# Norm and first FFN tiles worked by halves of the tokens behind three output projections, and a reordered opening

## What is computed

```python
x = x + 0.5 * swiglu(rms_norm(x, ffn1_norm), ffn1_w_in, ffn1_w_out)
h = rms_norm(x, mix_norm); ...attention...
x = x + mix @ w_mix_out                                  # output projection 1
x = x + 0.5 * swiglu(rms_norm(x, ffn2_norm), ffn2_w_in, ffn2_w_out)
for l in range(2):
    sh1, sc1, g1, sh2, sc2, g2 = split(silu(c) @ mod_w[l] + mod_b[l], 6)
    h = h + g1 * attention(modulate(rms_norm_2(h, norm1_g[l]), sh1, sc1))  # output projections 2, 3
    h = h + g2 * conv_ffn(modulate(rms_norm_2(h, norm2_g[l]), sh2, sc2))
```

## Time and profile before

| | |
|---|---|
| median of 3 runs | 2302.79 us (2302.18 to 2304.47) |
| profiled execution, its own time | 2299.5 us |
| its span, first to last instruction | 2298.0 us |
| PE busy (matmuls) | 2223.4 us, 97% of the span |
| DVE busy | 1270.5 us, 55% |
| ACT busy | 950.2 us, 41% |
| mean granted TensorE clock | 0.986 |

### The profile page before, as it was taken

One profiled execution on the slowest core, in us unless ns is written; L12 is line 12 of the kernel. 1 busy time (PEld: TensorE's weight loads), 2 busy tenths in 40 slices (PEclk: granted clock), 3 DMA queues, 4 the chain that ended last, 5 costly groups with the idle time before them and its releaser, 6 DMA issues.

```text
span 2298.0 us, 31235 instructions
## 1 busy us (share of the span) xinstructions
PE 2223.4 (97%) x11568; PEld 1831.8 (80%) x11568; DVE 1270.5 (55%) x2069; ACT 950.2 (41%) x1460; POOL 268.2 (12%) x442
## 2 busy tenths in 40 slices
PE   7999999998999999999999999999989999999998
PEld 6788887977778888887878788888878887888886
DVE  5754764456743363355356656456466655654654
ACT  4222223347644323324246554254253645533542
POOL 2110220035400020010036000000000430000000
PEclk9999999998999999999999999999999999999999
DMA  7864983231033283273321233333212012323332
GB/s 245 275 210 122 317 289 96 92 103 38 11 117 102 87 281 108 79 256 118 96 76 59 73 91 96 106 84 89 86 63 82 30 38 74 91 92 100 91 96 87
DMA packets 258720, 266.92 MB, mean 116 GB/s; under 512 B 8854, under 2 KB 201917, under 8 KB 258637
## 3 DMA queue, kind: packets, MB, share of 16 engines
q1 hardware_dynamic: 236909, 187.20, 27.2%
q0 software_dynamic: 21728, 78.63, 9.9%
HBM read 263.62 MB, written 12.66 MB: 120 GB/s over the span
## 4 chain that ended last, share of the span: by engine, by line
PE 86%; DVE 6%; ACT 4%; DMA 1%; POOL 1%; issue 1%; DVEq 0%; SPq 0%; POOLq 0%; ACTq 0%
PE bank L340 15%; PE bank L341 15%; PE bank L342 15%; PE bank L346 11%; PE bank L348 11%; PE bank L347 11%; PE bank L1567 2%; PE bank L1518 2%; PE bank L1542 2%; DVE w_lo L323 1%; ACT probs L1603 1%; POOL probs L1725 1%; DMA mod_w_more<-in_mod_w_dram 1%; PE bank L667 1%; DVE xT_lo L642 1%
## 5 line engine op out<-in xcount | busy, mean ns | idle before, releaser
L323 DVE TENSOR_TENSOR w_lo<-raw,w_hi 128x2048 fp32r<-128x2048 f32 (+3 forms) x202 | 415.6, 2057 | 374.2 <-ACT w_hi L319 371.5
L340 PE MATMUL bank<-xT_hi,w_hi 128*128 128x512 f32 x1560 | 609.6, 391 | 6.1 <-DVE xT_lo L642 4.2
L342 PE MATMUL bank<-xT_hi,w_lo 128*128 128x512 f32 x1560 | 607.8, 390 | 0.0
L341 PE MATMUL bank<-xT_lo,w_hi 128*128 128x512 f32 x1560 | 607.8, 390 | 0.0
L319 ACT ACTIVATE w_hi<-raw 128x2048 fp32r<-128x2048 f32 (+3 forms) x202 | 348.4, 1725 | 484.0 <-PE bank L348 429.9
L340 PEld LDWEIGHTS bank<-xT_hi,w_hi 128*128 128x128 f32 x1560 | 292.5, 188 | 73.3 <-DVE xT_lo L642 8.8
L342 PEld LDWEIGHTS bank<-xT_hi,w_lo 128*128 128x128 f32 x1560 | 292.5, 188 | 62.3
L341 PEld LDWEIGHTS bank<-xT_lo,w_hi 128*128 128x128 f32 x1560 | 292.4, 187 | 60.0
L346 PE MATMUL bank<-w_hi,hid_hi 128*128 128x512 f32 x704 | 277.8, 395 | 0.0
L347 PE MATMUL bank<-w_lo,hid_hi 128*128 128x512 f32 x704 | 277.8, 395 | 0.0
L348 PE MATMUL bank<-w_hi,hid_lo 128*128 128x512 f32 x704 | 277.7, 395 | 0.0
(11 more groups left out here) (303 smaller groups left out, 2858.8 us busy)
## 6 DMA issues: line engine op xcount, KB each, us to landing
raw<-in_ffn_w_in_dram SPq DMA_DIRECT2D x40, 1024.0 KB, 6.1
raw<-in_f_win_dram SPq DMA_DIRECT2D x40, 1024.0 KB, 6.0
mod_w<-in_mod_w_dram POOLq DMA_DIRECT2D x48, 512.0 KB, 5.3
mod_w_more<-in_mod_w_dram POOLq DMA_DIRECT2D x48, 512.0 KB, 5.6
raw<-in_ffn_w_out_dram SPq DMA_DIRECT2D x24, 768.0 KB, 4.5
raw<-in_f_wout_dram SPq DMA_DIRECT2D x24, 768.0 KB, 4.4
raw<-in_a_wqkv_dram SPq DMA_DIRECT2D x12, 1024.0 KB, 5.1
skewed_strips<-bias_strips POOLq DMA_DIRECT2D x32, 320.0 KB, 6.4
```

The lines of the kernel that those rows point to most:

```text
L323: dve.tensor_tensor(out=w_lo[:, slot, :n], in0=raw[:, slot, :n], in1=w_hi[:, slot, :n].bitcast(f32), op=ALU.subtract).then_inc(lo_done, 1)
L340: pe.matmul(o, lhsT=w[0], rhs=xs[0], start=first, stop=False)
L341: pe.matmul(o, lhsT=w[0], rhs=xs[1], start=False, stop=False)
L342: return pe.matmul(o, lhsT=w[1], rhs=xs[0], start=False, stop=last)
```

## The change

Four things change.

1. **Order in the second panel of an output projection.** PE does token tiles 0 and 1 with both chunks, then tiles 2 and 3 with the first chunk, then transposes the normed tiles 0 and 1, then tiles 2 and 3 with the second chunk.
2. **Norm in halves** (`HalfNorm`, for the norms behind the three projections). `xT` tiles are made 256 tokens wide, the first half (h = 0) inside the panel, the second behind it: sixteen evacuations in place of eight, each half as wide. On ACT the order is: split of the FFN's first chunk, four tiles of the first half, squares of token tile 2, four more tiles, squares of token tile 3, eight tiles of the second half.
3. **The first pair of these three FFNs by halves** (`by_halves`): gate and up tiles together over tokens 0 to 255, then PE transposes token tiles 2 and 3, then tokens 256 to 511; 96 matmuls of 256 columns in place of 48 of 512. The second half of an FFN's program is written out separately from the first.
4. **Opening.** A semaphore per `x` tile; ACT loads the table of the square root at once (`root_table`); the second weight chunk is loaded ahead of the constants; PE does `constants_pe` behind the first pair (DVE's copies of them move too), with eight extra matmuls (`BUSY`) ahead of the last transposes; DVE's bias strips move from the opening into the first half's output part.

The diff, cut to its core:

```diff
+                    if self.n == 0 and t == KT - 1:
+                        for _ in range(BUSY):
+                            pe.matmul(self.banks[t][:, 0:P], lhsT=ident[:, :], rhs=ident[:, :], start=True, stop=True)
...
+            def half_pe(self, pe, h):
+                for s in (2 * h, 2 * h + 1):
+                    pe.wait_ge(n_xn, self.n + s + 1)
+                    for t in (0, 2, 1, 3, 4, 6, 5, 7):
+                        ins = pe.transpose(self.place(h, t)[:, s % 2 * P:(s % 2 + 1) * P], self.tile(s)[:, t * P:(t + 1) * P],
+                                           ident[:, :])
+                        if s % 2 and t // 2 % 2:
+                            ins.then_inc(n_T, 1)
...
+            def half_act(self, act, h, ts):
+                for t in ts:
+                    hi = xT_hi[:, t, PAIR * h:PAIR * (h + 1)]
+                    if t % 2 == 0 or self.shifts is None:
+                        act.wait_ge(n_T, self.t + 4 * h + self.bank_of(t) + 1)
+                    if self.shifts is None:
+                        if t // 2 % 2:
+                            self.lo_ready(act, h, t - 2)
+                        act.activation(hi, self.place(h, t), ACT.Identity, scale=self.gains[:, t:t + 1],
+                                       bias=zero[:, :]).then_inc(n_hi, 1)
+                        continue
...
+                def by_halves():
+                    pe.wait_ge(lo_done, self.pair_c(0, 0, 0) + 1)
+                    pe.wait_ge(pair_free[0], EVEN * 2 * self.n + 1)
+                    for part in range(2):
+                        if part:
+                            self.norm.half_pe(pe, 1)
+                        for kt in range(KT):
+                            self.norm.lo_ready(pe, part, kt)
+                            for b, done in enumerate((g_done, used)):
+                                last = feature_major(pe, bank[b][:, PAIR * part:PAIR * (part + 1)],
...
-                self.gemm.pe(pe, 1)
+                self.gemm.piece(pe, 1, 0, [0, 1])
+                self.gemm.piece(pe, 1, 1, [0, 1])
+                self.gemm.piece(pe, 1, 0, [2, 3])
+                norm.half_pe(pe, 0)
+                self.gemm.piece(pe, 1, 1, [2, 3])
+
+            def act(self, act, norm, between=None, gained=None):
+                self.gemm.split_act(act, 0)
+                if between:
+                    between(act)
+                c = self.gemm.panels[1][3]
+                next_hi(act, c)
+                for s in range(2):
+                    norm.stats_act(act, s)
+                next_hi(act, c + 1)
+                if gained is not None:
+                    act.wait_ge(*gained)
+                norm.half_act(act, 0, range(4))
+                norm.stats_act(act, 2)
+                norm.half_act(act, 0, range(4, KT))
+                norm.stats_act(act, 3)
+                norm.half_act(act, 1, range(KT))
...
+                if between:
+                    between(dve)
+                if modulate:
+                    modulate(dve)
+                c = self.gemm.panels[1][3]
+                next_lo(dve, c)
+                for s in range(2):
+                    add(1, s)
+                for s in range(2):
+                    norm.scale_dve(dve, s)
+                next_lo(dve, c + 1)
+                norm.half_dve(dve, 0, range(4))
+                for s in range(2, TOK):
+                    add(1, s)
+                norm.half_dve(dve, 0, range(4, KT))
+                for s in range(2, TOK):
+                    norm.scale_dve(dve, s)
+                norm.half_dve(dve, 1, range(KT))
...
-        norm_ffn1 = Norm(lambda s: [(x_in, 64), (cols_done, 1)], column("ffn1_norm", KT))
+        norm_ffn1 = Norm(lambda s: [(x_in[s], 16)], column("ffn1_norm", KT))
...
-            ffn1.pair_sp(sp, 0, 0, 0)
+            for u in range(2):
+                ffn1.pair_sp(sp, 0, 0, u)
             constants_load(sp)
...
-            norm_ffn1.part(pe, 3)
-            constants_pe(pe)
-            ffn1.pe(pe)
+            ffn1.pe(pe, constants_pe)
```

More of the change, by code:

```diff
@@ L746, in half @@
                 def half(h, done=0):
-                    for u in range(done, 2 if done else 0):
-                        self.pair_sp(sp, h, 0, u)
                     with sp.Fori(1 if done else 0, PAIRS2) as i:
@@ L765, in sp, with pe @@
                         half(h)
-            def pe(self, pe):
+            def pe(self, pe, between=None):
                 def tile(o, slot, lo, first=False):
                     for kt in range(KT):
-                        if first:
+                        if first and self.norm.parts == 1:
                             self.norm.part(pe, kt)
@@ new lines, in by_halves @@
+                def by_halves():
[8 more added lines that the diff above has]
+                                last = feature_major(pe, bank[b][:, PAIR * part:PAIR * (part + 1)],
+                                                     w_part(self.slot(0), (b * KT + kt) * P, P),
+                                                     xT_part(kt, PAIR * part, PAIR), kt == 0, kt == KT - 1)
+                                if part and kt == KT - 1:
+                                    last.then_inc(done, 1)
@@ new lines, in half @@
+                def half(h, first=False):
+                    if first:
+                        if self.norm.parts == 2:
+                            by_halves()
+                        else:
+                            pair(h, 0, 0)
+                        if between:
+                            between(pe)
+                        pair(h, 0, 1)
+                    with pe.Fori(1 if first else 0, PAIRS2) as i:
+                        for u in range(2):
+                            pair(h, i, u)
@@ L809, in pe @@
                             last.then_inc(used, 1)
+                half(0, True)
+                half(1)
             def act(self, act):
@@ L914, in one, with half @@
                             mod_columns(dve, k)
-                with dve.Fori(0, 2) as h:
-                    with dve.Fori(0, PAIRS2 - 1) as i:
+                def half(h, first=None, later=None):
+                    if first:
+                        one(h, 0, 0, first)
+                        one(h, 0, 1)
+                    with dve.Fori(1 if first else 0, PAIRS2 - 1) as i:
                         for u in range(2):
@@ L970, in dve @@
                         add(TOK - 1)
+                if first:
+                    half(0, first, later)
+                    half(1)
+                else:
+                    with dve.Fori(0, 2) as h:
+                        half(h)
         class TokenGemm:
@@ new lines, in dve, with add @@
+            def dve(self, dve, norm, between=None, modulate=None):
+                def add(p, s):
+                    self.gemm.wait(dve, p, s)
+                    xs = x[:, s, p * SEQ:(p + 1) * SEQ]
+                    if self.gate is None:
+                        ins = dve.tensor_tensor(out=xs, in0=bank[4 * p + s][:, :], in1=xs, op=ALU.add)
+                    else:
+                        dve.tensor_tensor(out=full[:, s % 2, :], in0=bank[4 * p + s][:, :],
+                                          in1=self.gate.dst[:, p * SEQ:(p + 1) * SEQ], op=ALU.mult).then_inc(gated, 1)
+                        dve.wait_ge(gated, self.gated + TOK * p + s + 1)
+                        ins = dve.tensor_tensor(out=xs, in0=full[:, s % 2, :], in1=xs, op=ALU.add)
+                    ins.then_inc(self.gemm.free[s][0], 1)
@@ L2081, in dve @@
                 if self.gate is not None:
                     self.gate.done(dve)
[L2083 to L2099 removed]
+                self.gemm.split_dve(dve, 0)
@@ new lines, in dve @@
+                for s in range(TOK):
+                    add(0, s)
+                if between:
+                    between(dve)
[9 more added lines that the diff above has]
+                norm.half_dve(dve, 0, range(4))
```

168 lines of the change are left out of this document (92 added, 76 removed).

## The result

| | before | after |
|---|---|---|
| median of the runs, us | 2301.1 (20 runs, 2295.52 to 2304.47) | 2307.34 (20 runs, 2304.61 to 2311.66) |
| after / before, with its 95% interval | | 1.0031 (1.0024 to 1.0037) |
| profiled execution: own time, span, us | 2299.5, 2298.0 | 2306.48, 2305.0 |
| mean granted clock | 0.986 | 0.984 |

A forecast was written before the change was run, and what follows sets the result against it. The kernel was taken as bound by PE. Waits for weights +7.8, clock +6.8 and opening -4.8 gave +9.8 on 2299.5, 2309.3; with 3.3 to the median, 2312.6 us. Likeliest range 2308 to 2317, overall 2303 to 2318.

The forecast's parts named there:

- The likeliest case: Whole kernel: new waits and their clock cost outweigh the opening's gain; 2312.6 us, range 2308 to 2317, chance 0.55.
- the step from execution to median: Whole kernel: the median of the runs, 2302.8, lies 3.3 us above the profiled execution, added to the sum.
- Waits for weights take the place of waits for the norm: Output projections: of 15.5 us to be won none comes through, as PE then stands at weights; together +7.8 us.
- The stall in out_2: Out_2's second panel: PE wants the second chunk earlier, but ACT splits it behind the rotary tables; 4.9 us wait.
- The pairs' waits: Second pair of three FFNs: chunk split behind the norm's last tile and a table load; waits 3, 3.9, 3.9 us.
- The intervals: From the second panel's first matmul to the FFN's second pair: out_1 +2.1, out_2 +5.3, out_3 +0.4 us.
- The clock: Behind the four new PE waits the granted clock drops, 1.7 us each: +6.8, bounds 0 and 6.8.
- The rival of 0.17: Behind the four waits: same waits, but the clock stays up; +3.0, 2305.8 us, chance 0.17.
- The opening: Kernel start: first FFN matmul at 18.3 instead of 24.21, second pair -6.0; net -4.8 us, bounds -3 and -7.5.
- passed on: First FFN: DVE's copies of the constants, 1.2 us, delay PE in full, DVE already being 1.16 us late there.
- The rival "faster": Second pairs: norm's last tile 3 to 4 us sooner, PE runs straight on; -6.5, 2296.3 us, chance 0.12.
- The table load: ACT, ahead of the second pair's split: taken as 1.28 us from the trace, not the skill's 2.66.

The follow-up runs named there:

- run 5: The changed kernel with out_2's second panel chunk split ahead of the rotary tables; 1.0011 of before, 4.6 us less than after.
- run 4: The changed kernel with the second pair's chunk split earlier and the first pairs written out ahead of the loop; 0.9968 of before, 14.5 us less than after.
- run 3: The changed kernel with ten extra 128x128 matmuls filling each of the three waits for the second pair's chunk; 1.0011 of before, 4.6 us less than after.
- run 8: The changed kernel with the first norm waiting for all four tiles of x before squaring the first; single run, 2308.72 us.
- Run 11: The changed kernel with the three FFNs' first pairs written out ahead of the loop, split left in place; 1.0005 of before, 6.0 us less than after.
- run 1: The changed kernel with parts 1 to 3 undone, so the new opening alone; 0.9972 of before, 6.4 us less.
- run 2: The changed kernel with part 4 undone, so the halves alone with the old opening; 1.0072 of before, 16.6 us more.
- run 9: The changed kernel with both split moves (second pair's chunk, out_2's second chunk) and the first pairs written out, but the old opening; 0.9966 of before.
- run 6: The changed kernel with both split moves (second pair's chunk, out_2's second chunk) and the first pairs written out; 0.995 of before, repeated 0.9937.

## Why the prediction was right, and where it was off

The forecast was 2312.6 us and +9.8 against the profiled execution; measured were +7.0 in the profiled executions and 2307.34 in the median, inside the range and on the side forecast. The likeliest case is the one that came, but just below its own range of 2308 to 2317. The median is 5.3 us below the forecast. Of that, 2.8 us are in the sum, where two terms are off in opposite directions (the opening by 3.9 us, the clock by 1.8), so that it comes as near as it does partly by luck; the rest is the step from execution to median, taken as 3.3 us from three runs, which in the longer series is 1.6 for before and 0.9 for after (2301.1 against 2299.5, 2307.34 against 2306.48).

- *Waits for weights take the place of waits for the norm.* Right, at all four places. The stall in out_2: 4.9 predicted, 4.81 measured, and run 5 removes it by order alone. The pairs' waits: 3, 3.9 and 3.9 predicted, 2.96, 3.58 and 3.59 measured; run 4 removes them.
- *The intervals.* +2.1, +5.3 and +0.4 predicted; +2.3, +5.0 (7.6 without its 2.6 of clock) and 0.0 measured. Together 7.3 against 7.8. The prediction calls its 7.8 a loss at full clock, and takes the 6.8 and 6.5 us beyond PE's work in out_2 and out_3 for waits. It did not see that 1.4 and 1.6 us of these were clock already, so at full clock on both sides the loss is some 2.3, 6.4 and 1.6 us, 10.3 in all, and the change's net price in the clock is 8.6 - 3.0 = 5.6.
- *The clock*, +6.8 as 4 x 1.7 with 6.8 as upper bound: the mechanism was right (run 3), the size too small. Out_1 and out_3 lost 1.7 and 1.5, but out_2's two pauses 2.6 and 2.8, 8.6 in all, over the bound. The term took one row for the price of every pause. Out_2's stall alone cost 2.6 to 2.9 us in six of the seven traces that have it, and 1.6 in run 8. The Trainium skill ("TensorE: Matmul & The Clock Gate", section "What's actually happening") says that the count of slow matmuls varies from run to run; these traces agree, with 1.7 us in most places and 2.6 to 3.0 in some, and with one and the same pause costing 1.7 us in one execution and nothing in the next.
- *The clock stays up behind short pauses.* The rival of 0.17 built on the 2.22 us that cost nothing, and the prediction weighed it against the 2.40 us that cost 1.7. The other traces have the same two pauses, and there is no border between them. The first (2.21 to 2.28 us) costs 1.7 us in seven of the thirteen traces and nothing in six; the second, 2.40, likewise. In run 5 it is the first that costs, and behind the second the clock is 1.00 (lines below). Run 11 lost 1.7 us behind a pause of 2.15. The rival still failed here, since all fifteen unfilled pauses of 2.96 to 3.60 us cost something.
- *The opening*, -4.8 with -7.5 as bound: this is the term that was mis-sized most, with 8.7 us gained in the two profiled executions (7.2 by all the traces, below, and 6.4 by the time of run 1). The start was right, 18.3 predicted and 18.69 measured, and so nearly was the second pair's: -6.0 predicted, -6.3 measured (36.82 and 30.54). Two parts of the sum failed. The 1.2 us "passed on" at the fourth pair did not come: after has no wait there, and neither have runs 2 and 9, with the old opening (run 4, with the new one, has 0.48). That the wait of 1.16 us belongs to the kernel and not to one execution was assumed and is not so. And the clock's half of 1.7 was all of it: 0.72 in the first pair before, 1.00 now (windows from 24 to 30 us). The transposes for the norm behind the first FFN start between 384.3 and 385.7 in the eight executions that have the new opening unchanged (385.0 in the mean), and between 391.7 and 392.8 in the three with the old (392.2): 7.2 us. By that moment after was 8.5 us early (384.32 against 392.78), so 1.2 of it are the chance of these two executions.
- *The rival "faster"*, in which the chunk comes so much sooner that PE runs on, gave -0.9, -3.7 and -3.7 for the three places without the stall. Run 6 is that case, made by hand: -0.8, -2.9 and -3.0. So the rival priced rightly what a chunk that is ready is worth. What kept it from happening was the written order and the table load; that ACT's tiles could have been fast enough for it by themselves, no run shows.
- *The table load.* Taken as 1.28 us from the rows; after shows 1.28 again, with the split beginning 0.02 us behind its end (675.81 and 677.11), so the 2.66 us of the Trainium skill ("ScalarE: Activation LUTs", section "What ACT_TABLE_LOAD costs") are not borne out here either.

Run 5 behind its 2.22 us of idle, to be held against the earlier trace rows:

```profile
1714.73 0.50 PE L340 MATMUL bank<-kv_hi,w_hi 128*128 128x512 f32 x1 [2.22 <-DVE k_lo L1253]
...
1716.00:1718.00 2.00, 2.00 (x7) 1.57 (x6) 1.17 (x2) 0.60 (x1) 0.00 (x0) 0.57 1.03 420
1718.00:1720.00 2.00, 2.00 (x7) 1.57 (x6) 0.40 (x1) 0.60 (x1) 0.00 (x0) 0.58 0.17 64
```

The sum with what was measured: 7.3 (intervals) + 8.6 (clock) - 8.7 (opening, as these two executions have it) = 7.2, against 7.0 in the spans.

## What to carry to other kernels

Packing the bound engine's work closer gains only what the engines that feed it can follow: before such a move, list what the bound engine wants next, and when each item is ready, weights included, and not only for the operation that is moved. Where an item is late, look for its place in the feeding engine's own idle time; here two moved splits, with the first pair written out ahead of the loop, turned a loss of 0.72% (run 2) into a gain of 0.34% (run 9). A wait of TensorE ahead of its next work has a second price in the clock behind it. In the thirteen traces every pause of 2.57 us or more cost 1.4 to 3.0 us that way, pauses of 1.5 to 2.4 us cost 1.5 us or more in some executions and nothing in others, and single pauses of 1.2 to 1.36 us cost nothing. So a wait is worth halving even where it can't be removed.

## What the hardware showed beyond that

- The same pause of the same program part costs the clock in one execution and not in the next. PE's 1.64 us ahead of the transposes for the norm behind the first FFN are in all thirteen traces: seven lose 1.7 us behind them (after among them, clock 0.79, 0.50 and 0.86 in the windows from 384 to 390 us), six nothing (run 1, 1.00 in all three). For the 2.2 and 2.40 us of the earlier trace rows it is seven and six as well.
- Short pauses close together can cost as much as a long one: before loses 3.0 us behind 1.04, 0.98 and 0.95 us of idle within 6 us (from 1676 us on).
- Behind 3.58 us ahead of out_2's second pair 2.8 us went in after, but 1.7 behind 3.59 in run 5, where the stall some 40 us earlier was gone. The stall does not explain it: run 8 has the stall too, and lost 1.7 us behind the pair's pause of 3.58. What picks 1.7 or 2.8 stays open.
- The first attention takes 254.7 to 256.0 us, from the norm's first transposes to out_1's second panel, in eight of the executions (before and after, and runs 1, 2, 5, 8, 9 and 11), and 260.0 to 261.4 in the other five, with the granted clock between 480 and 540 us at 0.74 to 0.76 in place of 0.80 or more. Kernels with the same instructions up to there fall on both sides (after and run 3), so the edits don't explain it; what picks the one or the other stays open. It is not far from the distance between the lowest and the highest runs of one kernel (7 us in 20 runs of after), and why a single execution can't be used for differences of 5 us.
- The ACT program with the first pairs inside the loop has 48 table loads in the FFNs; with those of three FFNs written out there are 3 in all, and ACT's busy time falls from 955.1 to 893.9 us (run 6). Outside the three places where ACT is waited for, no time came of it that the runs show.
